# Forgetting attention: the causal mask added by VectorE, and the softmax denominators from products with a column of ones

## The chip, the cores and the metric

The kernel runs on one core of one Trainium2 chip. The metric is the device time of one execution in microseconds (us). The engines are TensorE (PE, with its weight loads shown as PEld), VectorE (DVE), ScalarE (ACT), GpSimd (POOL) and SyncE (SP), which issues the transfers. Each engine works through its own list of instructions in order and waits at semaphores for the others.

## What is computed

One step of a hybrid encoder layer: a joint input projection, three mixers side by side (attention with forgetting, a state space model, attention to a memory), and an output projection. The change touches the two attentions of the prompt, 2048 positions:

```python
def fox_block(q, k, v, cq, ck, q_pos, k_pos):          # 8 heads of 64
    s = jnp.einsum('bqhd,bkhd->bhqk', q, k).astype(jnp.float32) * (HEAD_DIM ** -0.5)
    s = s + jnp.swapaxes(cq, 1, 2)[..., :, None] - jnp.swapaxes(ck, 1, 2)[..., None, :]
    mask = k_pos[None, :] <= q_pos[:, None]
    p = jax.nn.softmax(jnp.where(mask, s, -jnp.inf), axis=-1)
    return jnp.einsum('bhqk,bkhd->bqhd', p.astype(v.dtype), v)

def memory_attention(q, mk, mv):                       # 4 heads of 64, 256 tokens, no mask
    s = jnp.einsum('bqhd,bkhd->bhqk', q, mk.astype(q.dtype)).astype(jnp.float32) * (HEAD_DIM ** -0.5)
    p = jax.nn.softmax(s, axis=-1)
    return jnp.einsum('bhqk,bkhd->bqhd', p.astype(q.dtype), mv.astype(q.dtype))
```

## The kernel before

The kernel has three stages: the projections with the state space model and the sample's attention (0 to 784 us of the profile), the prompt's attention (to 1218 us) and the output projection. The attention and the output projection are one function, `attention_and_output`.

**Units and cycles.** The attention is cut into units of four query tiles (128 positions each). A head has six: `fox` with the first query tile 0, 4, 8 and 12, and two `mem` units, in the order fox 0, fox 4, mem, mem, fox 8, fox 12. A fox unit has as many key blocks as lie at or before its last tile (4, 8, 12, 16), a mem unit two. For every key block there is a score block: 128 keys on the partitions, up to 4 x 128 queries along the columns, in one PSUM bank. In the last four key blocks of a fox unit the block on the diagonal is masked and the tiles before it are left out, so that these have 4, 3, 2 and 1 query tiles. Four score blocks are a cycle (`CYCLE`), 88 cycles in all, 11 to a head. Of those, four are on the diagonal: the first of the head (fox 0), the third (fox 4), the seventh (fox 8) and the eleventh (fox 12).

**The order.** `attention_order` writes one list of steps; every engine runs the steps of that list that concern it, in the list's order. In a cycle these are: `scores` of its four blocks, `exp` of them, four `top` steps, `row` where it is due, `both` and `add`, `den` of the units that ended two or more cycles before, `values` of the four blocks, `copied`.
- `scores` (TensorE, lines 2500 to 2506): two products per block into one bank (float32r, 2500 and 2505), the second of which brings in the forgetting terms and the negated maximum of each query. On the diagonal a third between them (2502) adds the mask: the triangle `causr` as weights, the identity `identr` as moving side, 128 columns.
- `exp` (ScalarE, 2633): the exponential of the whole bank into `pt` (`probs_turned`) in SBUF.
- `top` (TensorE 2482 and 2485, VectorE 2837 to 2856): the scores of a later unit the other way round, queries on the partitions, and their maximum.
- `row` (TensorE 2494, ScalarE 2622): these maxima turned into a row and written into the operands of the score products.
- `add` and `both` (GpSimd and VectorE, 2805, 2807, 2865): sums over the key blocks of a unit, still 128 partial sums for each query, one per partition.
- `den`: TensorE turns the four 128x128 float32 sums with the identity (2513), VectorE sums each over its 128 columns into `den` (2871) and takes the reciprocal (2875).
- `values` (TensorE, 2531): values times probabilities, full float32, 64 columns of weights, two tiles side by side.

**Banks.** Two PSUM banks hold the sums of `values`. The other six go round (`Ring`): each `scores`, `top`, `row` and `den` step takes the bank that was taken longest ago, and TensorE waits, in `tensor_steps`, for the one that empties it (`emptied`): for a score block the exponential, for a top VectorE's maximum, for a row the copy, for a denominator VectorE's reduction.

**The start.** GpSimd fills the constants (1782 to 1792) and TensorE waits for all of them (`CONSTS`) before its first instruction.

**Full float32.** A product of two float32 operands appears in the trace as two weight loads and two products. The state space model has such products too; line 1031 issues six per call of its step, 128x128 weights by 136 columns.

## Time and profile before

| | us |
|---|---|
| median of 3 runs | 1409.5 (1409.11 to 1409.52) |
| the profiled execution | 1408.32 |
| its span | 1406.4 |
| busy in the span: TensorE / VectorE / ScalarE / GpSimd | 1369.0 / 922.0 / 636.6 / 575.6 |
| TensorE's granted clock, mean share of full | 0.997 |

A line of the timeline has the start (us from the span's start), the length, the engine, the line of the kernel, what is written from what, the form (partitions x columns) and how many instructions it merges. What TensorE takes for a product in a row of products is the distance of the starts, not the length of one: lengths hold a latency that the next product covers. A group by line gives busy us, the mean ns of one, and the idle time just before it with what ended it.

### The profile page before, as it was taken

The page shows a single profiled execution, that of the slowest core. Times are in us where ns is not written, and L with a number is a line of the kernel's source. Part 1 is how long each engine was busy: PE and PEld are TensorE (multiplying, and loading weights), DVE is VectorE, ACT ScalarE, POOL GpSimd, SP SyncE. Part 2 cuts the span into 40 slices and gives each one's busy share as a digit, 9 for nine tenths or more (in the row PEclk, how much of TensorE's full clock was granted, in tenths as well). Part 3 has the DMA queues.
Part 4 walks back from the last instruction along what each step waited for, and adds up shares of the span by engine and source line. Part 5 has one row for each costly group of instructions (what it writes and reads, how often), then busy time and mean ns, then how long its engine had stood idle before and what let it go on. Part 6 is the DMA issues. An engine that isn't in the chain of part 4 may idle for free.

```text
span 1406.4 us, 25060 instructions
## 1 busy us (share of the span) xinstructions
PE 1369.0 (97%) x8382; PEld 1086.1 (77%) x8382; DVE 922.0 (66%) x2025; ACT 636.6 (45%) x1364; POOL 575.6 (41%) x606
## 2 busy tenths in 40 slices
PE   8999999999999999999999999999999999999998
PEld 7999767788877777777777777777777777778886
DVE  3789755593376778666433676776776776497775
ACT  6766423332353354445333455555555655422121
POOL 2122442200033234221100556877977867644452
PEclk9999999999999999999999999999999999999999
DMA  7885699987349769787998767448458355556552
GB/s 234 295 281 199 201 268 252 275 273 228 113 139 272 248 223 266 243 266 237 313 321 264 170 189 158 107 98 181 103 109 181 83 114 196 160 169 199 191 177 89
DMA packets 211023, 284.21 MB, mean 202 GB/s; under 512 B 49809, under 2 KB 146481, under 8 KB 207409
## 3 DMA queue, kind: packets, MB, share of 16 engines
q1 hardware_dynamic: 209856, 282.61, 68.7%
q8 instruction: 69, 1.13, 0.3%
q14 instruction: 58, 0.47, 0.1%
q10 hardware_dynamic: 1040, 0.00, 0.0%
HBM read 191.12 MB, written 90.19 MB: 200 GB/s over the span
## 4 chain that ended last, share of the span: by engine, by line
PE 60%; DVE 3%; POOL 2%; ACT 2%; issue 2%; DMA 2%; SPq 1%; DVEq 0%; ACTq 0%; POOLq 0%
PE in_g L927 14%; PE attn_pv L2531 10%; PE attn_s L2601 6%; PE attn_s L2500 6%; PE attn_s L2505 5%; PE attn_pv L2601 5%; PE attn_s L2485 5%; PE attn_s L2513 2%; PE in_b L1102 1%; POOL in_hv L1810 1%; PE in_b L1054 1%; PE attn_s L2554 1%; PE attn_s L2502 1%; PE in_b L1157 1%; PE in_b L1122 1%
## 5 line engine op out<-in xcount | busy, mean ns | idle before, releaser
L927 PE MATMUL in_g<-in_wh,in_xh 128*128 128x512 f32 (+2 forms) x904 | 331.4, 380 | 6.2 <-ACT in_xh L1219 2.4
L927 PE MATMUL in_g<-in_wl,in_xh 128*128 128x512 f32 (+2 forms) x904 | 321.9, 369 | 0.0
L2807 POOL TENSOR_TENSOR attn_probs<-attn_probs,attn_probs_turned 128x512 f32<-128x512 f32 (+3 forms) x200 | 214.3, 1072 | 64.9 <-ACT attn_probs_turned L2633 40.9
L927 PE MATMUL in_g<-in_wh,in_xl 128*128 128x512 f32 (+2 forms) x904 | 236.4, 380 | 1.4 <-DVE in_xl L1532 1.3
L2847 DVE TENSOR_REDUCE attn_tops<-attn_s 128x1 f32<-128x512 f32 (+3 forms) x288 | 159.1, 596 | 108.6 <-PE attn_s L2485 108.6
L2633 ACT ACTIVATE attn_probs_turned<-attn_s 128x512 f32<-128x512 f32 (+1 forms) x352 | 161.2, 545 | 125.7 <-PE attn_s L2505 124.8
L927 PEld LDWEIGHTS in_g<-in_wh,in_xh 128*128 128x128 f32 x904 | 165.5, 189 | 40.8 <-issue 7.4
L927 PEld LDWEIGHTS in_g<-in_wl,in_xh 128*128 128x128 f32 x904 | 165.6, 189 | 27.9
L927 PEld LDWEIGHTS in_g<-in_wh,in_xl 128*128 128x128 f32 x904 | 159.1, 190 | 34.9 <-issue 5.3
L1808 POOL TENSOR_SCALAR in_hs<-in_hs 128x8 f32<-128x8 f32 (+1 forms) x53 | 19.5, 368 | 401.8 <-DVE in_hs L1559 401.8
L2531 PE MATMUL attn_pv<-attn_probs_turned,attn_v 128*64 128x256 f32 (+1 forms) x1216 | 142.1, 363 | 0.0
L1219 ACT ACTIVATE in_xh<-in_xu 128x512 fp32r<-128x512 f32 x174 | 99.6, 623 | 55.6 <-DMA in_xu<-scratch_xt 50.4
L2531 PEld LDWEIGHTS attn_pv<-attn_probs_turned,attn_v 128*64 128x64 f32 x1216 | 84.7, 136 | 41.2 <-issue 7.5
L1532 DVE TENSOR_TENSOR in_xl<-in_xu,in_xh 128x512 fp32r<-128x512 f32 x106 | 68.6, 688 | 35.7 <-ACT in_xh L1219 35.1
L1810 POOL TENSOR_TENSOR in_hv<-in_hs,all_neghalf 128x8 f32<-128x8 f32 (+1 forms) x53 | 85.4, 1611 | 4.4
L1260 ACT ACTIVATE in_x_turned<-in_tr 128x512 fp32r<-128x512 f32 (+1 forms) x53 | 27.6, 520 | 87.2 <-PE in_tr L949 78.9
L2805 POOL TENSOR_TENSOR attn_probs<-attn_probs_turned 128x512 f32<-128x512 f32 x40 | 52.7, 1327 | 30.4 <-ACT attn_probs_turned L2633 30.4
L2505 PE MATMUL attn_s<-all_x,all_y 100*128 100x512 f32 (+3 forms) x160 | 61.2, 382 | 1.6 <-ACT all_x L2622 1.6
L2500 PE MATMUL attn_s<-attn_qa,attn_ka 128*128 128x512 f32 (+3 forms) x160 | 62.1, 388 | 0.0
L2500 PE MATMUL attn_s<-all_x,all_y 128*128 128x512 f32 (+3 forms) x160 | 62.0, 388 | 0.0
L2505 PE MATMUL attn_s<-attn_qb,attn_kb 100*128 100x512 f32 (+3 forms) x160 | 61.2, 383 | 0.0
L1579 DVE TENSOR_TENSOR in_work<-in_g,in_hr 128x512 f32<-128x512 f32 (+1 forms) x53 | 31.4, 593 | 38.3 <-POOL in_hr L1813 37.2
(377 smaller groups left out, 2685.8 us busy)
## 6 DMA issues: line engine op xcount, KB each, us to landing
in_xu<-scratch_xt SPq DMA_DIRECT2D x87, 512.0 KB, 5.4
in_xl<-scratch_xt SPq DMA_DIRECT2D x34, 512.0 KB, 4.6
in_raw<-in_w_in SPq DMA_DIRECT2D x40, 256.0 KB, 5.2
scratch_xt<-in_xu SPq DMA_DIRECT2D x19, 512.0 KB, 4.4
scratch_xt<-in_xl SPq DMA_DIRECT2D x17, 512.0 KB, 5.0
scratch_k<-in_x_turned SPq DMA_DIRECT2D x17, 512.0 KB, 7.2
scratch_q<-in_x_turned SPq DMA_DIRECT2D x17, 512.0 KB, 5.4
in_x_turned<-in_x_prompt SPq DMA_DIRECT2D x16, 512.0 KB, 4.8
```

The costliest lines, as they stand in the source:

```text
L927: last = X.matmul(g_ps[b][:, 0:m], x, ws[:, c, w0:w0 + m], start=(c == 0 and h == 0 and ws is wh), stop=(c == KC - 1 and h == 1))
L1219: F(xh[:, item_visit[j] % 2, 4 * h:4 * h + 4, :], xu[:, j % 2, 4 * h:4 * h + 4, :], ACT.Copy)\
L1532: V.tensor_tensor(xl[:, v % 3, 4 * h:4 * h + 4, :], xu[:, j % 2, 4 * h:4 * h + 4, :], fl(xh[:, v % 2, 4 * h:4 * h + 4, :]), ALU.subtract). ...
L1810: G.tensor_tensor(hv[:, 0:m], hs[:, 0:m], K.neghalf[:, 0:m], ALU.pow).then_inc(s_hchain, 1)
L2485: last = X.matmul(bank[:, at:at + n, :], qb[h][0:LANE, q], kb[h][0:LANE, keys], start=True, stop=True)
L2500: X.matmul(bank[:, part:, :], y2[h][:, keys], x2[h][:, q], start=True, stop=False)
L2505: X.matmul(bank[:, part:, :], y1[h][0:FULL, keys], x1[h][0:FULL, q], start=False, stop=True)\
L2531: last = X.matmul(v_ps[u.n % 2][lane * HD:(lane + 1) * HD, tiles[0] // 2:EACH // 2, :], vals[:, k, :], pt[:, s % SLOTS, tiles[0]::2, :], s ...
L2601: last = X.matmul(y_ps[at], ms[left][:, c, :], ws, start=(begins and c == 0 and k == 0), stop=(ends and c == HALF - 1 and k == 2))
L2633: F(pt[:, s % SLOTS, at:, :], ring_ps[ring.at["scores", s]][:, at:, :], ACT.Exp).then_inc(s_exp, 1)
L2807: E.tensor_tensor(acc[:, part:, :], acc[:, part:, :], mine, ALU.add).then_inc(added[engine], 1)
L2847: done = V.tensor_reduce(top_parts[:, d, i, 1 + k // 4:2 + k // 4], bank[:, 0:whole, :].rearrange("p n k -> p (n k)"), AX.X, ALU.max)
```

## The change

The mask's product leaves `scores`. A new step `mask`, one for each masked block, stands in the order between a diagonal cycle's `scores` and its `exp`: VectorE waits for the scores and adds the turned triangle `causal_turned` (a new bf16 constant) to the 128x128 block in PSUM, in place, and the exponential of such a block waits for VectorE and not for TensorE. `den` turns nothing: TensorE multiplies the four sums, as weights, with the column `K.one`, which gives four columns of one bank, and VectorE takes the reciprocal from there; the reduction, its tile and its semaphore are gone, and the bank is free after the reciprocal.

```diff
@@ -99,7 +99,7 @@
-CONSTS = 8
+CONSTS = 10
@@ -1782,14 +1782,17 @@
...
             G.memset(K.causal[:, :], 0.0).then_inc(s_const, 1)
+            G.memset(K.causal_turned[:, :], 0.0).then_inc(s_const, 1)
             G.memset(K.neghalf[:, :], -0.5).then_inc(s_const, 1)
             G.memset(K.one[:, :], 1.0).then_inc(s_const, 1)
-            pool.wait_ge(s_const, 5)
+            pool.wait_ge(s_const, 6)
             for of in (K.ident, K.identb):
...
                             base=0, pattern=[[-1, P]], channel_multiplier=1).then_inc(s_const, 1)
+            G.affine_select(out=K.causal_turned[:, :], in_=K.causal_turned[:, :], compare_op=ALU.is_ge, fill=MASKED,
+                            base=0, pattern=[[1, P]], channel_multiplier=-1).then_inc(s_const, 1)
             for what, *n in order:
@@ -1942,6 +1945,7 @@
...
         order += [("scores", b) for b in mine]
+        order += [("mask", b) for b in mine if scores[b][0].kind == "fox" and scores[b][1] >= scores[b][0].first]
         order += [("exp", b) for b in mine]
@@ -2106,7 +2110,6 @@
...
         top_parts = a.sb("tops", [P, 2, EACH, 5])
-        den = a.sb("den", [P, 2, EACH])
 
@@ -2149,7 +2152,8 @@
...
         s_score, s_exp, s_pv, s_copy = (a.sem(k) for k in ("scores", "exp", "values", "out_copied"))
-        s_addp, s_addv, s_den, s_denr, s_rden = (a.sem(k) for k in ("added_p", "added_v", "den", "den_read", "rden"))
+        s_addp, s_addv, s_den, s_rden = (a.sem(k) for k in ("added_p", "added_v", "den", "rden"))
+        s_masked, masks = a.sem("masked"), [x for x in order if x[0] == "mask"]
         s_store = [a.sem(f"stored{h}") for h in range(2)]
@@ -2214,7 +2218,7 @@
...
 
-            return {"scores": (s_exp, i + 1), "top": (s_top, i + 1), "row": (s_rowc, i + 1), "den": (s_denr, i + 1)}[what]
+            return {"scores": (s_exp, i + 1), "top": (s_top, i + 1), "row": (s_rowc, i + 1), "den": (s_rden, i + 1)}[what]
 
@@ -2498,8 +2502,6 @@
...
                     X.matmul(bank[:, part:, :], y2[h][:, keys], x2[h][:, q], start=True, stop=False)
-                    if u.kind == "fox" and k >= u.first:
-                        X.matmul(bank[:, part, :], causr[:, :], identr[:, :], start=False, stop=False)
                     if k == 0:
@@ -2510,7 +2512,7 @@
...
                     for i in range(EACH):
-                        last = X.transpose(bank[:, i, :], acc[:, i, :], K.ident[:, :])
+                        last = X.matmul(bank[:, 0, i:i + 1], acc[:, i, :], K.one[:, 0:1], start=True, stop=True)
                     last.then_inc(s_den, 1)
@@ -2578,7 +2580,7 @@
...
                     if q == 1 and j == 2:
-                        pe.wait_ge(s_denr, ALL)
+                        pe.wait_ge(s_rden, ALL)
                     if q > 1 and j == 2:
@@ -2624,7 +2626,10 @@
...
                     u, k, at = scores[s]
-                    act.wait_ge(s_score, s + 1)
+                    if ("mask", s) in masks:
+                        act.wait_ge(s_masked, masks.index(("mask", s)) + 1)
+                    else:
+                        act.wait_ge(s_score, s + 1)
                     if s >= SLOTS:
@@ -2855,6 +2860,11 @@
...
                                                 AX.X, ALU.max, negate=True).then_inc(s_neg, 1)
+                if what == "mask":
+                    u, k, at = scores[s]
+                    block = ring_ps[ring.at["scores", s]][:, at, :]
+                    dve.wait_ge(s_score, s + 1)
+                    V.tensor_tensor(block, block, K.causal_turned[:, :], ALU.add).then_inc(s_masked, 1)
                 if what == "add":
@@ -2866,13 +2876,9 @@
...
                     dve.wait_ge(s_den, s + 1)
-                    if s >= 2:
-                        dve.wait_ge(s_rden, s - 1)
-                    V.tensor_reduce(den[:, s % 2, :], ring_ps[ring.at[what, s]][:, :, :], AX.X, ALU.add).then_inc(s_denr, 1)
-                    dve.wait_ge(s_denr, s + 1)
                     at = u.first + (u.head % 2 * (MQ // P) if u.kind == "mem" else 0)
                     by = rmem[:, at:at + EACH, u.head // 2] if u.kind == "mem" else rfox[:, at:at + EACH, u.head]
-                    V.reciprocal(by, den[:, s % 2, :]).then_inc(s_rden, 1)
+                    V.reciprocal(by, ring_ps[ring.at[what, s]][:, 0, 0:EACH]).then_inc(s_rden, 1)
                 if what == "fold":
@@ -3011,7 +3017,8 @@
...
         D.rows_of = rows_of
-        K.ident, K.identb, K.causal = a.sb("ident", [P, P]), a.sb("identb", [P, P], BF16), a.sb("causal", [P, P], BF16)
+        K.ident, K.identb = a.sb("ident", [P, P]), a.sb("identb", [P, P], BF16)
+        K.causal, K.causal_turned = a.sb("causal", [P, P], BF16), a.sb("causal_turned", [P, P], BF16)
         K.neghalf, K.one = a.sb("neghalf", [P, FOX_HEADS]), a.sb("one", [P, 1])
```

## Rows read from the trace of the kernel before

**Rows 1.** The page's first part: engine, busy us (share of the span), instructions.

```profile
PE 1369.0 (97%) x8382; PEld 1086.1 (77%) x8382; DVE 922.0 (66%) x2025; ACT 636.6 (45%) x1364; POOL 575.6 (41%) x606
```

**Rows 2.** The page's chain that ended last: its share of the span by engine.

```profile
PE 60%; DVE 3%; POOL 2%; ACT 2%; issue 2%; DMA 2%; SPq 1%; DVEq 0%; ACTq 0%; POOLq 0%
```

**Rows 3.** Windows: stretch, length, busy us of each engine (instructions), clock, DMA share, GB/s.

```profile
792.00:1218.00 426.00, 423.99 (x2772) 316.85 (x2771) 295.80 (x774) 243.99 (x609) 324.34 (x283) 1.00 0.58 137
```

**Rows 4.** Timeline, TensorE, head 2's fox 4 diagonal cycle: start us, length us, instruction.

```profile
912.73 0.50 PE L2500 MATMUL attn_s<-all_x,all_y 128*128 128x512 f32 x1
913.06 0.22 PE L2502 MATMUL attn_s<-attn_identr,attn_causr 128*128 128x128 f32 x1
913.12 0.45 PE L2505 MATMUL attn_s<-all_x,all_y 100*128 100x512 f32 x1
...
914.50 0.97 PE L2485 MATMUL attn_s<-all_y,all_x 66*128 66x512 f32 x4
...
915.42 0.62 PE L2513 MATMUL attn_s<-all_ident,attn_probs 128*128 128x128 f32 x4
915.97 1.52 PE L2531 MATMUL attn_pv<-attn_probs_turned,attn_v 128*64 128x256 f32 x14
```

**Rows 5.** Timeline, ScalarE, the same cycle: the four exponentials.

```profile
913.60 1.43 ACT L2633 ACTIVATE attn_probs_turned<-attn_s 128x512 f32<-128x512 f32 x4 [3.32 <-PE attn_s L2505]
```

**Rows 6.** One line's instructions: the exponentials, xcount, ns min/median/max.

```profile
L2633 ACT ACTIVATE attn_probs_turned<-attn_s x352: 296/598/617, 794.7 to 1218.0; 128x512 f32<-128x512 f32 x144, 128x256 f32<-128x256 f32 x32
```

**Rows 7.** Timeline, weight loads where a diagonal cycle's products are narrow.

```profile
934.72 0.19 PEld L2502 LDWEIGHTS attn_s<-attn_identr,attn_causr 128*128 128x128 f32 x1
934.83 0.19 PEld L2505 LDWEIGHTS attn_s<-all_x,all_y 100*128 100x128 f32 x1
934.94 0.53 PEld L2485 LDWEIGHTS attn_s<-attn_kb,attn_qb 66*128 66x128 f32 x4
```

**Rows 8.** Groups by line: the mask's products, xcount | busy us, mean ns.

```profile
L2502 PE MATMUL attn_s<-attn_identr,attn_causr 128*128 128x128 f32 x128 | 30.2, 236 | 0.0
```

**Rows 9.** Timeline, TensorE, a denominator that stands alone in its cycle.

```profile
1104.89 0.60 PE L2513 MATMUL attn_s<-all_ident,attn_acc_v 128*128 128x128 f32 x4
1105.42 1.95 PE L2531 MATMUL attn_pv<-attn_probs_turned,attn_v 128*64 128x256 f32 x16
```

**Rows 10.** Timeline, TensorE: full float32 products, 128 weights, 136 columns.

```profile
333.81 1.61 PE L1031 MATMUL in_b<-s_room 128*128 128x136 f32 x12
```

**Rows 11.** One line's instructions, VectorE, 128x128 with an operand in PSUM: xcount, ns min/median/max.

```profile
L1711 DVE TENSOR_TENSOR in_late<-in_b,in_late x1: 286/286/286, 548.7 to 548.7; 128x128 fp32r<-128x128 f32 x1
```

**Rows 12.** Timeline, VectorE, into the fox 8 diagonal cycle (starts at 933.22).

```profile
933.52 0.68 DVE L2871 TENSOR_REDUCE attn_den<-attn_s 128x4 f32<-128x512 f32 x1
...
935.04 0.18 DVE L2875 RECIPROCAL attn_rmem<-attn_den 128x4 f32<-128x4 f32 x1
```

**Rows 13.** Timeline, TensorE: head 2's other diagonal cycles, starts and what waits for banks.

```profile
903.24 0.50 PE L2500 MATMUL attn_s<-all_x,all_y 128*128 128x512 f32 x1
...
905.99 0.44 PE L2531 MATMUL attn_pv<-attn_probs_turned,attn_v 128*64 128x256 f32 x2
...
933.22 0.50 PE L2500 MATMUL attn_s<-all_x,all_y 128*128 128x512 f32 x1
...
935.70 0.22 PE L2494 MATMUL attn_s<-attn_identr,attn_negmax 128*128 128x128 f32 x1
...
952.25 0.50 PE L2500 MATMUL attn_s<-all_x,all_y 128*128 128x512 f32 x1
...
954.89 0.34 PE L2494 MATMUL attn_s<-attn_identr,attn_negmax 128*128 128x128 f32 x2
...
956.61 0.50 PE L2500 MATMUL attn_s<-attn_qa,attn_ka 128*128 128x512 f32 x1
```

**Rows 14.** Timeline, the start of the kernel.

```profile
2.11 0.29 POOL L1791 TENSOR_SCALAR_AFFINE_SELECT all_causal<-all_causal 128x128 bf16<-128x128 bf16 x1
...
4.82 1.94 PE L882 MATMUL in_b<-all_ident,in_x_turned 128*128 128x128 f32 x8 [4.82 <-DMA in_x_turned<-in_x_sample]
```

## The prediction, on record before the change was run

> **What bounds the kernel now.** I read the page's busy shares first: TensorE is busy 97% of the span, VectorE 66%, and the chain that ended last runs 60% through TensorE and 3% through VectorE [rows 1, 2]. Then the windows by stage, because the change touches one stage only: the attention, from 792 to 1218 us. There TensorE is busy 423.99 of 426.00 us at full clock, VectorE 295.80, ScalarE 243.99 [rows 3]. So whatever TensorE stops doing there is gained and whatever it newly does is paid, unless a new wait opens; VectorE has 130 us to spare in that stage, but not at every moment. Last I read one cycle of four score blocks on the timelines, because the question is one of fractions of a microsecond in an order that repeats: head 2 runs from 903.24 to 956.61, 53.37 us [rows 13], and each head has eleven such cycles, four of them on the diagonal.
>
> **The mask's products (removed).** 128 products of the triangle with the identity go [rows 8], four in each of 32 diagonal cycles. What does one cost? Not its 236 ns, most of which is latency that the next product covers. In the narrow products of a diagonal cycle the starts of the weight loads stand 0.11 us apart (934.72, 934.83, 934.94) whatever the products behind them [rows 7]: a load of 128 columns every 0.11 us is the engine's pace there, and each mask product has a load of its own. Four of them are 0.44 us a cycle, and 32 cycles 14.1 us. The 1.77 us from the first score product to the first "top" (912.73 to 914.50) would become 1.33 [rows 4].
>
> **The mask on VectorE (added), with a new wait.** One 128x128 addition in PSUM per masked block stands between the scores and the exponential. The nearest row is an addition of that size with one operand in PSUM, 0.286 us, once [rows 11]; I take 0.29, plus 0.04 us for each of two semaphores instead of one (the exponential starts at 0.87 in the cycle, 0.03 after the scores end at 0.84 [rows 4, 5]). VectorE is free in time only if the queue ahead of it is short. In the fox 8 cycle it is not: two denominators hold it from 933.52 to 935.22, two microseconds into the cycle that starts at 933.22 [rows 12]. But the change takes out just those two reductions of 0.68 us, so that VectorE would be free some 1.4 us earlier, about 0.6 into the cycle. The two halves of the change need each other. Behind the mask on VectorE wait the tops of the same cycle, which start on TensorE only after the scores; they are hardly delayed.
>
> Who waits for the exponential? The values do, with room to spare: they start 3.24 us into the cycle [rows 4] and the exponentials end at 2.30 [rows 5]. But so do PSUM banks. Six banks go round among scores, tops, rows and denominators; worked out from the ring's rule, the third and fourth top of a cycle take the banks of its first and second score block, and what follows (a row, a denominator) those of the third and fourth. This slack is small. In the fox 4 cycle the exponentials end at 2.30 and the denominator that takes the last bank starts at 2.69 [rows 4, 5]. After the change: the first score block ends at 0.73 (its last product takes the mask's place at 0.33 and lasts 0.40), the mask ends at 0.73 + 0.04 + 0.29 = 1.06, the first exponential starts at 1.10, and the chain of four, 1.43 us long and paced by ScalarE itself [rows 5], ends at 2.53. TensorE can resume about 0.06 later, at 2.59. Without the wait it would be there at 2.69 - 0.44 = 2.25. So of 0.44 us only 0.10 is left. The other three kinds of diagonal cycle read the same way [rows 13]:
> - fox 12: the second of two rows takes the last bank; it starts about 2.70 (2.64 for the first) and would start at 2.59: 0.10 gained.
> - fox 8: a row takes the third block's bank. The last exponential is of one block, 0.296 us at the least of its line [rows 6], and starts before the third ends, so the third ends 0.1 to 0.2 before the chain: 2.42 with the resumption, against 2.48 now: 0.06 gained.
> - fox 0: only the second exponential holds a top; by the same count it ends near 2.07, that top starts at 2.13, and the values 0.33 later at 2.46 instead of 2.75: 0.29 gained.
> Together 0.55 us a head, 4.4 us; I take 4, since a later semaphore costs 0.05 in each. The bounds are 14.1 (no bank ever holds) and a loss of 3 (VectorE busy a little longer than I think).
>
> **The denominators on TensorE (changed).** Now: four turnings, 0.53 us from the first to the first value product (1104.89 to 1105.42) [rows 9]; their starts are 0.11 apart, so 0.44 of stream and 0.09 of changing to products of 64 columns. After: four products of the sums (128x128, float32) with one column of ones. One column streams in no time, but the sums are the stationary side. And a full float32 product is two records with a load each: the six calls that feed the window at 333.81 show as twelve, 1.61 us, at most 0.13 each at 136 columns [rows 10]. So a denominator is eight loads. The first is hidden under the top before it; seven at 0.11 are 0.77, with the change 0.86: +0.34 us (0.86 - 0.53, rounded up for the last load). Each head has four denominators alone in a cycle and two in one cycle, of which the second adds 8 x 0.11 - 0.44 = 0.44. Per head 5 x 0.34 + 0.44 = 2.14, times 8 is 17.1 us. At 0.13 a load [rows 10] it would be 0.47 and 0.60, 23.6 us; the lower bound is below nothing, -4 us, if one record did for a product of one column. I take 0.11, because load starts of that distance are what rows 7 show where nothing else holds TensorE.
>
> The Trainium skill's page "TensorE: Matmul & The Clock Gate" speaks both ways: by its section LDWEIGHTS a load of 128 columns takes 107 ns, as rows 7 have it, and by its Back-to-back issue gap a sustained pair of load and product takes about 81 ns at 128 columns, which no row here shows. By the second the sum would be that of rival 5.
>
> **The rest.** VectorE loses 48 reductions of 0.68 us and gains 128 additions of 0.29: +4 us on an engine with 130 free, worth nothing by itself; its reciprocals now read PSUM and free the bank sooner, also worth nothing, since no product waits for it today. GpSimd makes one more constant (a fill and a selection, 0.29 each at most): it ends its constants at 2.40 and TensorE starts at 4.82 on a load from memory [rows 14], so 0.6 us are hidden; with the cover gone they would cost 0.6. The tail only has one denominator among its products, in the 17.1 above.
>
> **Sum.** 17.1 - 4 = +13 us. The profiled execution took 1408.32 us (span 1406.4), 1.2 below the median of 1409.5; both would move by the same: 1421.3 for the profile, 1422.5 for the median.
>
> **Rivals.**
> 1. The banks don't hold (TensorE finds its bank free in spite of the later exponential). Then 17.1 - 14.1 = +3: 1412.5. For it: the slack of 0.39 in rows 4 and 5 is real. Against: 0.44 of earliness plus 0.23 of lateness is more than 0.39. 10%.
> 2. The small products are cheap (the other side, faster): a product with one column is one record. Then a denominator is four loads, 3 x 0.11 + 0.09 = 0.42, 0.11 less than now, and in a pair nothing more: -4 us, and with the mask's -4 the kernel takes 1401. It decides from the point where a denominator costs less than 0.61 us (now 0.53, plus 4/48 that the mask gives back). Against: all full float32 products I read come in twos [rows 10]. 9%.
> 3. The small products are dear: a load can't overlap the product before it, so each takes its 0.19 [rows 7]: 8 x 0.19 + 0.09 is 1.08 more than now, 48 times 52 us, 1457. Against: rows 7 show 0.11 between loads of 0.19. 8%.
> 4. VectorE comes late to the mask, by half a microsecond in each of 32 cycles: +16, 1438. Rows 12 speak for it, the removed reductions against it. 6%.
> 5. Pairs of load and small product run at 0.08 us instead of 0.11. Then a denominator is 7 x 0.08 + 0.09 = 0.65 (+0.12), the second of a pair +0.20, a head +0.8, eight +6.4; less 4, 1412. 7%.
> The pace of rival 5 is that of the Trainium skill's "TensorE: Matmul & The Clock Gate", Back-to-back issue gap.
>
> **How the numbers follow.** The forecast, two loads per product at 0.11 to 0.13 with most of the mask's gain lost to banks, has 60%; its own range is 1416 to 1430. The range 1410 to 1437 takes in rivals 1 and 5 and most of 4's way and leaves out 2 and 3. Measurement can tell about 0.2%, 2.8 us. Faster by more: rival 2 and a little of 1: 0.10. Within: the lower halves of 1 and 5: 0.10. Slower: 0.80.
>
> **What would show it.** After the change the denominators' line should have 384 products instead of 192, their load starts 0.11 apart, about 0.87 us from the first to the first value product. A diagonal cycle should reach its first top after 1.33 us, and tops, rows and the fox 4 denominator should now show waits for the exponential's line. Head 2 should take about 55.0 us instead of 53.37. The mask's row should read near 0.29 us. Wrong would be: 192 products at that line (rival 2), starts 0.19 or 0.08 apart (3, 5), no waits for banks and the whole 0.44 gained in each diagonal cycle (1), or first exponentials later than 1.3 us into a cycle (4).

## The result and the profile after

The changed kernel takes 1434.3 us (median of 4 runs, 1433.1 to 1434.75) against 1409.3 us (4 runs, 1406.65 to 1409.52): a ratio of 1.018, with a 95% interval of 1.0163 to 1.0198. It is slower by 25 us. Forecast were 13 us more, with a range up to 1437: the direction and the range held, the size was half of what came. Head 2 takes 56.08 us; forecast was about 55.0.

| us | before | after |
|---|---|---|
| the profiled execution's span | 1406.4 | 1432.5 |
| busy: TensorE / VectorE | 1369.0 / 922.0 | 1393.3 / 921.5 |
| TensorE's granted clock, mean share of full | 0.997 | 0.992 |
| head 2, first score product to the next head's | 53.37 | 56.08 |

The page's busy shares of the changed kernel come first, then its chain that ended last.

```profile
PE 1393.3 (97%) x8446; PEld 1103.7 (77%) x8446; DVE 921.5 (64%) x2105; ACT 637.1 (44%) x1364; POOL 572.8 (40%) x608
...
PE 57%; DVE 4%; DMA 3%; issue 2%; ACT 2%; POOL 1%; SPq 1%; ACTq 0%; DVEq 0%; POOLq 0%
```

Against [rows 1, 2]: TensorE still is the bound, with 24.3 us more of busy time in a span that is 26.1 us longer. It has 64 instructions more, and that number says what happened: 128 mask products less, 192 records more in the denominators. The groups by line of the changed kernel show both halves (columns: the group, its count, then busy us and mean ns of one, then the idle time before it).

```profile
L2867 DVE TENSOR_TENSOR attn_s<-attn_s,all_causal_turned 128x128 f32<-128x128 f32 x128 | 32.2, 294 | 34.4 <-PE attn_s L2507 33.0
...
L2515 PE MATMUL attn_s<-all_one,attn_probs 128*128 128x1 f32 x256 | 30.7, 245 | 0.0
L2515 PEld LDWEIGHTS attn_s<-all_one,attn_acc_v 128*128 128x128 f32 x128 | 16.7, 191 | 1.6 <-ACT attn_probs_turned L2638 0.3
L2515 PE MATMUL attn_s<-all_one,attn_acc_v 128*128 128x1 f32 x128 | 15.3, 240 | 0.0
```

The denominators are 256 + 128 = 384 products of one column, two for each of the 192 calls, and every one has a weight load of its own, as forecast. The mask takes 294 ns on VectorE; forecast were 0.29 us.

Now the fox 4 diagonal cycle of head 2, the one of [rows 4, 5]. These are lines of the changed kernel's timeline (start us, length us, instruction): TensorE, ScalarE, VectorE.

```profile
920.82 0.50 PE L2504 MATMUL attn_s<-all_x,all_y 128*128 128x512 f32 x1
...
922.17 1.12 PE L2489 MATMUL attn_s<-all_y,all_x 66*128 66x512 f32 x4
923.24 0.33 PE L2498 MATMUL attn_s<-attn_identr,attn_negmax 128*128 128x128 f32 x1
923.41 1.05 PE L2515 MATMUL attn_s<-all_one,attn_probs 128*128 128x1 f32 x8
924.39 0.87 PE L2533 MATMUL attn_pv<-attn_probs_turned,attn_v 128*64 128x256 f32 x7
...
921.93 1.43 ACT L2638 ACTIVATE attn_probs_turned<-attn_s 128x512 f32<-128x512 f32 x4 [3.89 <-DVE attn_s L2867]
...
921.60 1.10 DVE L2867 TENSOR_TENSOR attn_s<-attn_s,all_causal_turned 128x128 f32<-128x128 f32 x4 [1.12 <-PE attn_s L2507]
```

The first top starts 1.35 us into the cycle, not 1.77: the four mask products are gone. The exponentials start at 1.11 instead of 0.87 and wait for VectorE. So the denominator starts at 2.59, where it was 2.69: of 0.42 us gained at the start of the cycle 0.10 are left. And the values start 0.98 behind the denominator, where it was 0.55. In the cycle before this one, where the denominator waits for no bank, it is 0.88 (2.87 to 3.75), forecast was 0.87. The 0.10 more of this cycle is the denominator's first load: its first two products start 0.13 us apart, in the cycle without the wait 0.03. The forecast had that load hidden under the product before it; here it is not. So far it goes nearly as forecast. Two things do not. One shows in the last diagonal cycle of the head (fox 12), which starts at 962.22: GpSimd, VectorE, ScalarE and TensorE of the changed kernel's timeline (the bracket is the idle time before an instruction and what ended it).

```profile
956.03 8.93 POOL L2812 TENSOR_TENSOR attn_probs<-attn_probs,attn_probs_turned 128x512 f32<-128x512 f32 x6
...
962.08 1.75 DVE L2812 TENSOR_TENSOR attn_acc_v<-attn_acc_v,attn_probs_turned 128x512 f32<-128x512 f32 x1
963.75 0.88 DVE L2867 TENSOR_TENSOR attn_s<-attn_s,all_causal_turned 128x128 f32<-128x128 f32 x4
...
964.07 1.43 ACT L2638 ACTIVATE attn_probs_turned<-attn_s 128x512 f32<-128x512 f32 x4 [1.85 <-DVE attn_s L2867]
...
964.72 0.88 PE L2489 MATMUL attn_s<-attn_kb,attn_qb 66*128 66x128 f32 x2 [0.47 <-ACT attn_probs_turned L2638]
```

An addition of VectorE's share of the running sums stands ahead of the masks and takes 1.75 us beside GpSimd's additions. The first mask starts 1.53 us into the cycle instead of 0.78, and TensorE stands still for 0.47 us until an exponential gives back a bank. The cycle takes 5.04 us, before it took 4.36 [rows 13].

The other is the clock. Behind denominators it falls four times in the attention: behind the pair of heads 1, 3 and 7, and once more in head 1. These are windows of the changed kernel (stretch, length, busy us of PE, PEld, DVE, ACT and POOL with their instructions, granted clock, DMA share, GB/s), around the cycle of head 1 that has the pair of denominators.

```profile
876.00:880.00 4.00, 4.00 (x24) 3.13 (x20) 1.50 (x5) 2.07 (x4) 2.09 (x2) 1.00 0.00 0
880.00:882.00 2.00, 2.00 (x18) 1.71 (x19) 1.97 (x8) 0.00 (x0) 1.73 (x2) 0.91 0.00 0
882.00:884.00 2.00, 2.00 (x10) 0.76 (x8) 0.58 (x3) 0.00 (x0) 0.00 (x0) 0.50 0.00 0
884.00:886.00 2.00, 2.00 (x12) 1.76 (x10) 0.67 (x3) 0.39 (x1) 0.00 (x0) 0.74 0.00 0
886.00:888.00 2.00, 2.00 (x16) 1.33 (x15) 2.00 (x12) 1.75 (x7) 1.57 (x2) 1.00 0.00 0
```

TensorE is busy throughout, and still the clock falls to 0.50, which is 1.2 of 2.4 GHz. What it did before stands in its timeline: sixteen products of one column.

```profile
879.25 1.84 PE L2515 MATMUL attn_s<-all_one,attn_probs 128*128 128x1 f32 x16
881.02 3.12 PE L2533 MATMUL attn_pv<-attn_probs_turned,attn_v 128*64 128x256 f32 x16
```

The sixteen products of values behind them take 3.12 us; in a cycle at full clock sixteen take 1.95 [rows 9].

Not every fall comes from there. One stands in the first cycle of head 0, before any denominator of the attention, behind a stretch in which TensorE was idle for 1.69 of 4 us. Two windows of the changed kernel:

```profile
790.00:794.00 4.00, 2.31 (x13) 1.97 (x12) 3.36 (x11) 2.87 (x8) 3.82 (x3) 0.86 0.17 65
794.00:798.00 4.00, 4.00 (x20) 3.00 (x20) 2.96 (x5) 1.47 (x6) 3.57 (x4) 0.50 1.04 224
```

That cycle takes 9.01 us, before it took 6.60. But the same fall is in the profiles of kernels without one-column products (the mask alone, 8.51 us; the best of the halves, 9.16), so it isn't the denominators'. And the profiled execution of the kernel before has a fall elsewhere, at 250 to 260 us (granted clock 0.66, 1.00 in the changed kernel), and between 222 and 260 us it loses 3.1 us against the changed one. Such falls trade places between executions; only those behind denominators are laid to the change here.

### The profile page after: what moved, and what is told of

It is laid out like the page before. It is cut to its first block, busy times and chain, and to the rows that moved or that the text cites. A ratio compares the mean times of both kernels' runs of the same rounds, so it can differ in the third digit from the quotient of the medians.

```text
span 1432.5 us, 25226 instructions
## 1 busy us (share of the span) xinstructions
PE 1393.3 (97%) x8446; PEld 1103.7 (77%) x8446; DVE 921.5 (64%) x2105; ACT 637.1 (44%) x1364; POOL 572.8 (40%) x608
## 4 chain that ended last, share of the span: by engine, by line
PE 57%; DVE 4%; DMA 3%; issue 2%; ACT 2%; POOL 1%; SPq 1%; ACTq 0%; DVEq 0%; POOLq 0%
PE in_g L927 12%; PE attn_pv L2533 10%; PE attn_s L2603 6%; PE attn_s L2504 6%; PE attn_s L2489 5%; PE attn_s L2507 5%; PE attn_pv L2603 5%; PE attn_s L2515 3%; DMA in_xu<-scratch_xt 2%; PE in_b L1102 1%; POOL in_hv L1813 1%; DVE attn_negmax L2842 1%; PE in_b L1054 1%; DVE attn_acc_v L2812 1%; SPq L777 1%
## 5 line engine op out<-in xcount | busy, mean ns | idle before, releaser
L2533 PE MATMUL attn_pv<-attn_probs_turned,attn_v 128*64 128x256 f32 (+1 forms) x1216 | 147.9, 374 | 0.0
L2507 PE MATMUL attn_s<-all_x,all_y 100*128 100x512 f32 (+3 forms) x160 | 56.9, 370 | 1.7 <-ACT all_x L2624 1.7
L2507 PE MATMUL attn_s<-attn_qb,attn_kb 100*128 100x512 f32 (+3 forms) x160 | 57.5, 374 | 0.0
```

What stands on the lines that cost most here:

```text
L2507: X.matmul(bank[:, part:, :], y1[h][0:FULL, keys], x1[h][0:FULL, q], start=False, stop=True)\
L2533: last = X.matmul(v_ps[u.n % 2][lane * HD:(lane + 1) * HD, tiles[0] // 2:EACH // 2, :], vals[:, k, :], pt[:, s % SLOTS, tiles[0]::2, :], s ...
```

## The experiments

The account that the experiments test: the denominators of one-column products cost 2.1 us a head for their loads, as in the prediction, the mask gains almost nothing, and what is missing is the late VectorE and the clock. The ratios are to the kernel before as it ran beside each experiment; its median went from 1406.3 to 1409.3 us, so the ratios compare better than the times. Where heads or cycles are compared, it is the distance from one cycle's first score product to the next one's, in the profiled executions. "Alone" is a denominator that is the only one of its cycle.

**The mask alone.** VectorE adds the mask, the denominators stay as they were.

```diff
-                    if u.kind == "fox" and k >= u.first:
-                        X.matmul(bank[:, part, :], causr[:, :], identr[:, :], start=False, stop=False)
...
+                if what == "mask":
...
+                    V.tensor_tensor(block, block, K.causal_turned[:, :], ALU.add).then_inc(s_masked, 1)
```

> The mask added by VectorE, the denominators still turned by TensorE and summed by VectorE. Theory (TensorE is early by 0.44 us in a diagonal cycle but waits for banks that the later exponentials hold, and VectorE comes late where its queue is long): the fox 0 cycle 0.2 us shorter, fox 4 0.1, fox 12 between 0.1 shorter and 0.7 longer, and the fox 8 cycle about 1.1 longer, because two reductions of 0.68 us stand ahead of the masks and the first exponential starts near 2.3 us instead of 0.88. Per head +0.7 to +1.5, in all 6 to 12 us slower: 1415 to 1421. Rival (what the mask's products cost is gained, and all of the change's loss is the denominators'): 1395 to 1405, and the first exponential of fox 8 near 1.1.

Measured: 1417.49 us against 1407.53, ratio 1.0065 (1.004 to 1.009), as expected. The fox 8 diagonal cycle, which starts at 937.41 in head 2, takes 5.25 us instead of 4.08. Timeline of this kernel, VectorE, ScalarE, TensorE:

```profile
938.52 0.68 DVE L2882 TENSOR_REDUCE attn_den<-attn_s 128x4 f32<-128x512 f32 x1
939.24 0.18 DVE L2886 RECIPROCAL attn_rmem<-attn_den 128x4 f32<-128x4 f32 x1
939.34 0.87 DVE L2868 TENSOR_TENSOR attn_s<-attn_s,all_causal_turned 128x128 f32<-128x128 f32 x4
...
939.64 1.43 ACT L2639 ACTIVATE attn_probs_turned<-attn_s 128x512 f32<-128x512 f32 x4 [4.48 <-DVE attn_s L2868]
...
940.29 0.88 PE L2490 MATMUL attn_s<-attn_kb,attn_qb 66*128 66x384 f32 x2 [0.65 <-ACT attn_probs_turned L2639]
```

The two reductions hold VectorE until 1.9 us into the cycle, the masks wait behind them, and TensorE waits 0.65 us for a bank. This is what the prediction said of the two halves needing each other: with the reductions gone, the same masks start at 0.77. In the other cycles the gains are small: fox 0 0.17 (heads 1 to 6), fox 4 0.08 (head 3 loses 0.07), fox 12 0.06 in heads 2 to 4 and 0.02 in head 1, while in heads 0, 5 and 6 fox 12 is 0.22 to 0.25 longer. In the first two cycles of head 0 this profile is 3.0 us longer than that of before; a fall of the clock stands there (the one named above).

**The denominators alone.** One column of ones, the mask still on TensorE; VectorE's reduction is gone as in the changed kernel.

```diff
-                        last = X.transpose(bank[:, i, :], acc[:, i, :], K.ident[:, :])
+                        last = X.matmul(bank[:, 0, i:i + 1], acc[:, i, :], K.one[:, 0:1], start=True, stop=True)
```

> The denominators as products with the column of ones, the mask still a product on TensorE. Theory (eight weight loads of 0.11 us in place of four turnings, and a lower clock after the pair of denominators in some heads): +0.35 in a cycle with one, +0.8 with two, 2.2 a head, 17 to 18 us, plus up to 6 us of clock: 1426 to 1433. Rival A (the two parts hurt only together): within 5 us of the kernel before, 1409 to 1414. Rival B (the lower clock comes from the waits that the mask brings, not from these products): 1426 to 1427 with full clock throughout the attention.

Measured: 1432.16 us (1428.54 to 1438.73), ratio 1.0181 (1.0148 to 1.0213), about what the whole change costs. The profile is of the slowest of the four runs. Heads 2, 4 and 6 are 2.20, 2.21 and 2.22 us longer than before, at full clock: 0.34 to 0.37 for each of four denominators alone, 0.83 for the pair. Heads 1, 3, 5 and 7 are longer by 3.8 to 5.5 us, since the clock falls in them behind the pair (in head 1 once more), without any mask on VectorE. So neither rival holds. Windows of this kernel:

```profile
880.00:890.00 10.00, 10.00 (x58) 7.61 (x58) 3.81 (x11) 3.17 (x7) 4.25 (x4) 0.83 0.00 0
890.00:900.00 10.00, 9.68 (x59) 6.87 (x58) 7.91 (x25) 6.63 (x19) 9.55 (x9) 1.00 0.02 7
900.00:910.00 10.00, 10.00 (x59) 6.60 (x58) 5.53 (x16) 4.80 (x12) 8.39 (x7) 0.83 0.07 23
```

The runs of this kernel stand in the order of their clocks: the four had mean clocks of 0.990, 0.991, 0.993 and 0.994, and took 1438.73, 1433.46, 1430.86 and 1428.54 us. But the clock is not all of it: by estimate, 0.004 less of mean clock is 11 us more at half speed, which costs at most 6 of the 10 us between the slowest and the fastest. What the rest is was not looked for.

**One product in place of four.** This prices a load by itself: the changed kernel, but each denominator has the product of its first tile only.

```diff
-                    for i in range(EACH):
+                    for i in range(1):
                         last = X.matmul(bank[:, 0, i:i + 1], acc[:, i, :], K.one[:, 0:1], start=True, stop=True)
```

> The changed kernel with one product with the column of ones per denominator instead of four; the other three tiles' denominators are left out (they take the first one's). Theory (each product is two weight loads of 0.11 us): six loads fewer in each of 48 denominators, 0.66 us each, 32 us less than the changed kernel, and no fall of the clock, up to 6 us more: 1396 to 1403. Rival (a fixed price per denominator, such as changing over, and not the loads): less than 10 us gained, 1424 to 1434.

The other three tiles of a unit get the first one's denominator. Measured: 1396.68 us against 1406.33, ratio 0.9927 (0.9902 to 0.9951), 37.6 us under the changed kernel, as expected. At the denominators' line this kernel has:

```profile
L2515 PEld LDWEIGHTS attn_s<-all_one,attn_probs x64: 186/190/192, 803.6 to 1181.8; 128*128 128x128 f32 x64
...
L2515 PEld LDWEIGHTS attn_s<-all_one,attn_acc_v x32: 186/188/192, 832.7 to 1210.4; 128*128 128x128 f32 x32
```

96 loads for 48 calls: two to a call. In undisturbed heads a cycle with a denominator alone is 0.65 to 0.69 us shorter than in the changed kernel, for six loads less; the cycle with the pair 1.33 to 1.38, for twelve: 0.11 us for each load and its product in both. That is the price the prediction took; rivals 2, 3 and 5 fall. Loads and products go away together here; that it isn't the products' columns shows below, where 64 times as many cost next to nothing. No clock falls behind a pair in this kernel.

By the Trainium skill, "TensorE: Matmul & The Clock Gate", section LDWEIGHTS, a load takes its number of columns divided by 1.2 in ns, 107 for 128: the distance of the load starts agrees, 0.11 us; the length of one in the trace is 0.19. The 81 ns for a load and its product of its section Back-to-back issue gap is not what these loads show.

**No mask at all.** The kernel before without the mask's products and with a triangle of zeros: the causal mask is missing from the computation.

```diff
                     X.matmul(bank[:, part:, :], y2[h][:, keys], x2[h][:, q], start=True, stop=False)
-                    if u.kind == "fox" and k >= u.first:
-                        X.matmul(bank[:, part, :], causr[:, :], identr[:, :], start=False, stop=False)
```

> The kernel before without the causal mask: its product is left out and the triangle is all zeros, so this part of the computation is missing. Theory (a mask product costs the 0.11 us of its weight load, and a bank is free in time if the exponential needn't wait for VectorE): the first top 1.33 us into a diagonal cycle instead of 1.78, 0.44 gained in each of 32, 14 us: 1395. Rival A (it costs only the 0.06 us of its own 128 columns): 7 to 8 us, 1402. Rival B (the banks bind even without the mask on VectorE, since TensorE comes 0.44 earlier): 1402 to 1409.

Measured: 1397.53 us against 1407.53, ratio 0.993 (0.9912 to 0.9947): 10 us, about 1.2 a head, not 14: between what the theory and what its rivals expected. In fox 4 the four products give 0.42 us, 0.11 each. That is all the mask could give if VectorE were free of cost. The fox 4 and fox 12 diagonal cycles give 0.42 and 0.40, fox 0 0.31 to 0.35, and fox 8 nothing. Why not fox 8? The timeline of this kernel, TensorE in that cycle (from 926.24), shows it:

```profile
927.60 0.27 PE L2485 MATMUL attn_s<-attn_kb,attn_qb 66*128 66x128 f32 x1
928.08 0.80 PE L2485 MATMUL attn_s<-attn_kb,attn_qb 66*128 66x256 f32 x3 [0.21 <-DVE attn_den L2869]
```

The second top takes the bank of the second denominator, and VectorE still reads it: the bank comes free 1.8 us into the cycle whatever TensorE saved before. The prediction did not look at that bank. (Before, this top starts at 1.89, so the bank was just free.) In the changed kernel the reductions are gone, and there the second top starts at 1.45.

**64 columns of ones.** Does the clock fall because a product of one column gives the array so little to do? The loads are the same, the products 64 columns wide.

```diff
-                        last = X.matmul(bank[:, 0, i:i + 1], acc[:, i, :], K.one[:, 0:1], start=True, stop=True)
+                        last = X.matmul(bank[:, i, 0:64], acc[:, i, :], K.one[:, 0:1].to_broadcast([P, 64]), start=True, stop=True)
...
-                    V.reciprocal(by, ring_ps[ring.at[what, s]][:, 0, 0:EACH]).then_inc(s_rden, 1)
+                    V.reciprocal(by, ring_ps[ring.at[what, s]][:, 0:EACH, 0]).then_inc(s_rden, 1)
```

> The changed kernel with 64 columns of ones instead of one in each denominator product (the same column read 64 times). Theory (the weight load of 0.11 us sets the pace, and 64 columns of full float32 stream in half of that; the clock fell because the products with one column leave TensorE nearly idle for 0.9 to 1.7 us): the denominators take the same time, within 0.05 us each, the clock stays at full through the attention, and the kernel is 4 to 6 us faster than the changed one: 1428 to 1430. Rival A (the clock falls because of the waits for banks and VectorE): the same dips, 1434. Rival B (the products' own columns add to the loads): 0.05 us more in each of 384 products, 20 us, 1450.

Measured: 1428.99 us (1427.45 to 1429.96), ratio 1.0149 (1.0129 to 1.017), 5.3 us less than with one column, though TensorE streams 64 times as many columns. The intervals of the two ratios overlap (1.0163 to 1.0198 for one column), but no run of one does with a run of the other: four of 1433.1 to 1434.75 at mean clocks of 0.991 and 0.992, four of 1427.45 to 1429.96 at 0.996 to 0.999. The window of the fall, and the timeline at the same pair, in this kernel:

```profile
880.00:890.00 10.00, 10.00 (x69) 7.71 (x68) 6.96 (x29) 4.29 (x12) 6.64 (x7) 1.00 0.01 2
```

```profile
880.03 1.89 PE L2515 MATMUL attn_s<-all_one,attn_probs 128*128 128x64 f32 x16
881.85 1.95 PE L2533 MATMUL attn_pv<-attn_probs_turned,attn_v 128*64 128x256 f32 x16
```

The sixteen products take 1.89 us, 0.05 more, and the values behind them 1.95 instead of 3.12. No cycle with a pair is longer than 6.62 us in heads 1 to 7, where the changed kernel had 7.74, 7.63 and 7.55 in heads 1, 3 and 7. The clock does fall in the first cycle of head 0 here too, so it isn't full through the whole attention as expected.

**The same without the mask on VectorE.** To have the clock's part without the other half's.

```diff
-                        last = X.transpose(bank[:, i, :], acc[:, i, :], K.ident[:, :])
+                        last = X.matmul(bank[:, i, 0:64], acc[:, i, :], K.one[:, 0:1].to_broadcast([P, 64]), start=True, stop=True)
```

> The denominators alone, as in e2, but with 64 columns of ones as in e4. Theory (0.39 us a denominator for its loads and 64 columns, 0.86 for the pair, 2.4 a head; full clock): 19 us over the kernel before, 1425 to 1428, ratio 1.0135, and 5 us less than e2; what is left to e4 (ratio 1.0149) is the mask's part, 2 us. Rival (e4's gain over the changed kernel came from somewhere in the mask's part and not from the columns): as e2, 1430 to 1433, with a mean clock of 0.99.

Measured: 1426.32 us (1425.06 to 1427.1) against 1408.28, ratio 1.0129 (1.0112 to 1.0146), with mean clocks of 0.997 and 0.998 and no fall in heads 1 to 7. That is 5.8 us under the one-column kernel without the mask. With and without the mask on VectorE, then, 64 columns give back 5 to 6 us by the medians, 4 and 7 by the ratios. The mask's half costs what lies between 1.0129 and 1.0149, some 0.2%, 3 us, though the two intervals overlap.

**The additions behind the masks.** If the addition ahead of the masks makes them late in fox 12, then VectorE should do it after them. On top of the 64 columns:

```diff
         def vector_steps(dve, steps):
             V = nc.vector
+            steps, late, after = list(steps), [], []
+            diag = {x[1] // CYCLE for x in steps if x[0] == "mask"}
+            for x in steps:
+                if x[0] == "add" and x[1] // CYCLE + 1 in diag:
+                    late.append(x)
+                    continue
...
```

> The kernel of e4 (64 columns of ones), with VectorE's additions of the cycle before a diagonal one moved behind that cycle's masks in VectorE's list. Theory (in the fox 12 cycle the masks stand behind an addition of 128x512 in SBUF that takes 0.68 to 1.75 us): the first mask at 0.78 us in every fox 12 cycle instead of up to 1.5, that cycle 0.3 to 0.7 us shorter in six heads, 3 us in all, 1426 against 1429 of e4. Rival (the delayed additions come to stand before the tops and hold banks or the next cycle): the cycles after fox 12 grow by as much, 1429.

Measured: 1427.31 us (1426.59 to 1427.58), ratio 1.0148 (1.0133 to 1.0163), against 1.0149 of the 64 columns. The cause is right: the fox 12 cycles are 0.65 us shorter than with 64 columns in heads 2, 3 and 4, 0.29 in 0, 5 and 6, and their masks start at 0.78 in all. The gain is not kept. VectorE in this kernel, fox 12 of head 2 (from 958.09) and fox 0 of head 3 (from 962.38):

```profile
958.86 1.09 DVE L2878 TENSOR_TENSOR attn_s<-attn_s,all_causal_turned 128x128 f32<-128x128 f32 x4 [0.84 <-PE attn_s L2507]
959.86 1.74 DVE L2812 TENSOR_TENSOR attn_acc_v<-attn_acc_v,attn_probs_turned 128x512 f32<-128x512 f32 x1
...
963.53 0.91 DVE L2878 TENSOR_TENSOR attn_s<-attn_s,all_causal_turned 128x128 f32<-128x128 f32 x4
```

The addition of 1.74 us is now behind these masks and so ahead of the maxima and of the next masks, which start 1.15 us into their cycle: fox 0 is 0.30 to 0.36 longer in heads 3, 4 and 5. And one cycle of head 1 is 1.93 longer, in which TensorE waits for ScalarE and ScalarE for GpSimd. Behind that wait the clock falls:

```profile
888.00:892.00 4.00, 3.19 (x18) 1.99 (x14) 4.00 (x7) 1.28 (x3) 3.92 (x3) 1.00 0.00 0
892.00:894.00 2.00, 2.00 (x10) 1.34 (x10) 1.83 (x8) 1.42 (x3) 2.00 (x3) 1.00 0.36 135
894.00:896.00 2.00, 2.00 (x13) 1.21 (x14) 1.44 (x4) 0.00 (x0) 1.86 (x2) 0.60 0.00 0
```

So 64 columns do not keep the clock up in every case: TensorE had stood idle for 0.81 of 4 us, then came a denominator.

**The best of the halves.** The kernel before, with its denominators, and the mask on VectorE in the three kinds of cycle in which it gained something, additions moved as above.

```diff
+        order += [("mask", b) for b in mine if scores[b][0].kind == "fox" and scores[b][0].first != 8 and scores[b][1] >= scores[b][0].first]
...
-                    if u.kind == "fox" and k >= u.first:
+                    if u.kind == "fox" and u.first == 8 and k >= u.first:
                         X.matmul(bank[:, part, :], causr[:, :], identr[:, :], start=False, stop=False)
```

> The kernel before with the mask on VectorE in the fox 0, fox 4 and fox 12 cycles only (fox 8 keeps its product on TensorE), and the additions moved behind the masks as in e5; the denominators as before. Theory (what VectorE's mask brings is 0.17, 0.08 and 0.07 us in these cycles, once it isn't late, the rest of the 0.44 being held by banks): 0.3 us a head, 2 to 3 us faster than the kernel before, ratio 0.998. Rival (the moved additions cost elsewhere): no faster than before.

Measured: 1406.45 us (12 runs, 1403.86 to 1409.66) against 1406.33 (17 runs), ratio 0.9999 (0.9987 to 1.001): no difference. Fox 4 gains 0.08, fox 12 0.07, fox 0 0.15 to 0.18 in heads 1, 6 and 7, but in heads 2 to 5 it is 0.06 to 0.26 longer, behind the moved additions. No version that was run and leaves nothing out beats the kernel before.

## Why the prediction was right, and where its size was off

The changed kernel's profile against that of before is 26.1 us longer. By kinds of cycle it splits like this; the forecast was made of the first two lines.

| part | forecast | measured | from |
|---|---|---|---|
| denominators | +17.1 | +17.7 | 2.21 a head, heads 2, 4, 6 of the kernel with the denominators alone, times 8 |
| mask | -4 | about +1.5 | fox 0 -0.18 x 7, fox 4 -0.05 x 8, fox 8 +0.04 x 7, fox 12 +0.67 x 3 and +0.21 x 4 |
| clock behind denominators | 0 | about +5.7 | excess over full clock: head 1 3.2, head 3 1.5, head 7 1.0 |
| first cycle of head 0 | 0 | +2.4 | 9.01 - 6.60, a fall of the clock behind idle time |
| outside the attention | 0 | -1.7 | -2.1 ahead of it (before has a fall there), +0.4 behind it |

That is 25.6 us; the other 0.5 are not assigned. The last two lines belong to the two executions and not to the change.

- **The denominators: right.** Two records for a call, a load for each, 0.11 us a load, the first hidden (but in fox 4, where the wait for the bank lays it bare: 0.10 us). Forecast 0.34 alone and 0.44 more for the second of a pair; measured 0.34 to 0.37 alone and 0.83 for the cycle of the pair, 0.05 more than 0.34 + 0.44. The run with one product instead of four shows the price of a load and its product.
- **The mask off TensorE: right.** The first top at 1.34 to 1.36 in undisturbed diagonal cycles, forecast 1.33.
- **The bank's wait: right in kind and place, small in size.** The prediction worked out that the denominator of fox 4 would start at 2.59 and the row of fox 8 at 2.42; they start at 2.59 and 2.48, which for fox 8 is no gain. The top of fox 0 starts at 2.13 as forecast, but the values come 0.44 behind it and not 0.33, so of 0.29 only 0.18 were gained. Two readings fit: the top waited for its bank, so its own load of 0.11 is not hidden; or the values wait for the cycle's last exponential, which ends at 2.53, 0.04 before they start. The trace puts 0.25 us of the weight loads' idle time there to ScalarE, so that "with room to spare" does not hold for fox 0. Which of the two binds was not tested. The forecast set 0.55 a head; without the late VectorE fox 0, 4 and 8 give 0.19, and fox 12, where the masks are on time, 0.07 (the runs with the mask alone, and with the additions moved).
- **VectorE late: this step failed.** "VectorE is free in time only if the queue ahead of it is short" was followed for fox 8 alone, and there it was right: the mask alone loses 1.17 us in that cycle, and with the reductions gone 0.04. For fox 12 it was not asked. An addition is queued there too, and its length isn't a constant. The trace of before already showed that: another of VectorE's addition lines in it, all 128x512, runs from 683 to 1791 ns (shown in the last section). Rival 4 came true in one kind of cycle: the masks 0.75 us late in three heads and some 0.3 late in four, 2.9 us in all, and 0.7 that fox 12 should have gained. Its price was of the right order for a cycle (0.67 for 0.75 late), its count was not 32 but 7.
- **The clock: missing in the prediction.** It priced the stationary side rightly and said that one column "streams in no time". It never asked what a stretch of such products does to the granted clock. With turnings in the same place, each of 128 columns, the clock was 1.00 over the whole stage in the profiled execution [rows 3]. In the changed kernel the clock falls behind the pair in three heads of eight, and once behind a denominator alone that follows a wait for ScalarE. That the one-column products are the cause of these falls is shown by exchange: with the same loads and 64 columns the falls behind pairs are gone, twice, for 5.3 and 5.8 us, and the mean clock of each of the eight runs is above that of each of the eight with one column. Why some heads are spared and others not is open, and so are the falls that have nothing to do with denominators.
- **The range: held with some luck.** It reached to 1437 for the sake of rival 4, VectorE late by half a microsecond in all 32 cycles. That did not come; about 3 us of it did, and the falls of the clock, which no rival had, used the rest: 1434.3 of 1437. The forecast's own range, 1416 to 1430, was missed.

## What to carry to other kernels

A small product costs what its weights cost: before turning data is replaced by a product with a vector, count the loads, and in full float32 count them twice. When work moves to an engine that has time to spare, follow its queue in every kind of cycle where the moved step is due, and take the longest time of what stands ahead, not its mean. Part of what is taken off may come back as waits for buffers in any case: here 4 of 14 us with the mask left out altogether, and all of it with the mask on VectorE. And look at the granted clock behind a stretch of one-column products; here wider ones were the faster ones.

## What the runs showed of the hardware that was not expected

- **Wider products, less time.** 384 products of one column against 384 of 64, the loads the same: 1434.3 and 1429.0 us with the mask on VectorE, 1432.2 and 1426.3 without. At full clock a cycle with denominators is 0.03 to 0.06 us longer with the wide ones; the gain is in the clock. The Trainium skill, "TensorE: Matmul & The Clock Gate", section HAM oscillation, tells of a clock that falls behind idle gaps of TensorE. The fall in the first cycle of head 0 comes behind idle time, 1.69 of 4 us, though 1.51 of 4 in the kernel before brought none. Behind the pair of head 1 there is no gap: 4.00 of 4.00 and 2.00 of 2.00 us busy in the windows ahead of the fall. Busy with what, is the question that the busy time doesn't answer.
- **An addition of one size that takes 0.68 or 1.75 us.** VectorE's 128x512 float32 addition in SBUF takes 0.68 us at 952.11 of the kernel before and 1.75 us at 962.08 of the changed one, beside GpSimd's six additions of the same size (8.93 us, 1.49 each). In the traces of all ten kernels, none of VectorE's 104 additions of this size into its sums that ran without GpSimd took more than 0.70 us; every longer one had GpSimd at work beside it, as had 63 of the short ones. One line's instructions in the kernel before and one line's in the changed kernel, VectorE (count, then ns min/median/max):

```profile
L2805 DVE TENSOR_TENSOR attn_acc_v<-attn_probs_turned x16: 683/790/1791, 819.2 to 1206.6; 128x512 f32<-128x512 f32 x16
```

```profile
L2812 DVE TENSOR_TENSOR attn_acc_v<-attn_acc_v,attn_probs_turned x32: 414/922/1751, 826.3 to 1240.1; 128x512 f32<-128x512 f32 x24, 128x256 f32<-128x256 f32 x8
```

The Trainium skill, "SBUF — State Buffer", section Who interferes with whom, says that a VectorE instruction with two SBUF inputs contends with a GpSimd instruction that reads SBUF, and calls the shared pair of ports an exclusive lock. By estimate, a wait of up to one GpSimd addition, 1.49 us, on top of 0.68 would reach 2.17; the trace stays within it. No run took GpSimd's additions away, so this cause is argued, with the overlap for it, and not shown by exchange.
